# Two units of each attention's output projection beside the attention's end

## The reference, cut to what matters

```python
h = attention(x, ...)                     # concatenated heads o @ w_out, 1024 x 1024
x = layer_norm(ALPHA * x + h, g, b)       # ALPHA = 4 ** 0.25, over the 1024 features
f = conv_ffn(x, ...)
x = layer_norm(ALPHA * x + f, g, b)
```

## Time and profile before

| | us |
|---|---|
| median of 3 runs | 2278.91 |
| lowest, highest | 2278.16, 2282.58 |
| the profiled execution's own time | 2278.12 |
| its span in the trace | 2276.3 |
| PE busy | 2162.4 (95%) |
| mean granted clock of PE | 0.975 of full |

### The profile page before, as it was taken

One profiled execution on the slowest core, in us unless ns is written; L12 is line 12 of the kernel. 1 busy time (PEld: TensorE's weight loads), 2 busy tenths in 40 slices (PEclk: granted clock), 3 DMA queues, 4 the chain that ended last, 5 costly groups with the idle time before them and its releaser, 6 DMA issues.

```text
span 2276.3 us, 27949 instructions
## 1 busy us (share of the span) xinstructions
PE 2162.4 (95%) x10712; PEld 1797.8 (79%) x10720; DVE 1166.1 (51%) x1852; ACT 1005.5 (44%) x2029; POOL 945.9 (42%) x714
## 2 busy tenths in 40 slices
PE   7999899999999898899999999989999999999997
PEld 6888778888877787778888878777678887888886
DVE  3545565544335687565554354676854326444322
ACT  6656444444225666244443245656543334332221
POOL 4555564343447673543433443222413343322233
PEclk9999999999999999999999998999999999999998
DMA  4111122322222321222222212111012222222221
GB/s 176 42 56 58 54 93 95 108 95 102 89 88 79 98 84 38 75 74 93 93 101 94 102 58 75 38 38 38 19 65 93 97 97 72 95 98 106 86 102 54
DMA packets 29844, 183.06 MB, mean 80 GB/s; under 512 B 3984, under 2 KB 4112, under 8 KB 11920
## 3 DMA queue, kind: packets, MB, share of 16 engines
q1 hardware_dynamic: 29712, 181.27, 23.0%
HBM read 174.97 MB, written 2.10 MB: 78 GB/s over the span
## 4 chain that ended last, share of the span: by engine, by line
PE 83%; DVE 7%; ACT 4%; issue 3%; POOL 2%; DMA 1%; SPq 0%; POOLq 0%; DVEq 0%; ACTq 0%
PE PS L1492 81%; PE PS L1617 1%; DVE bQS L2232 1%; PE PS L1730 0%; POOL LO L2783 0%; DMA RAW<-wall 0%; ACT HI L1816 0%; DVE aQS L2232 0%; DVE T_f L2304 0%; DVE bP L2536 0%; DVE YH L2334 0%; PE PS L1665 0%; DVE XL L2309 0%; ACT bQS L2010 0%; POOL cROT L2858 0%
## 5 line engine op out<-in xcount | busy, mean ns | idle before, releaser
L2783 POOL TENSOR_TENSOR LO<-RAW,HI 128x512 fp32r<-128x512 f32 (+2 forms) x382 | 542.4, 1436 | 605.7 <-ACT HI L1816 605.7
L1492 PE MATMUL PS<-XH,HI 128*128 128x512 f32 (+1 forms) x1584 | 637.9, 403 | 23.4 <-DVE XL L2232 7.1
L1492 PE MATMUL PS<-XH,LO 128*128 128x512 f32 (+1 forms) x1584 | 626.0, 395 | 0.0
L1492 PE MATMUL PS<-XL,HI 128*128 128x512 f32 (+1 forms) x1584 | 620.2, 396 | 2.2 <-DVE XL L2309 2.1
L1816 ACT ACTIVATE HI<-RAW 128x512 fp32r<-128x512 f32 (+3 forms) x668 | 366.0, 607 | 171.2 <-PE PS L1492 168.0
L2232 DVE TENSOR_TENSOR LO<-RAW,HI 128x512 fp32r<-128x512 f32 (+2 forms) x286 | 302.5, 1062 | 246.3 <-ACT HI L1816 245.9
L1492 PEld LDWEIGHTS PS<-XH,HI 128*128 128x128 f32 (+1 forms) x1584 | 302.5, 191 | 86.5 <-issue 20.7
L1492 PEld LDWEIGHTS PS<-XH,LO 128*128 128x128 f32 (+1 forms) x1584 | 301.7, 190 | 65.7 <-issue 0.8
L1492 PEld LDWEIGHTS PS<-XL,HI 128*128 128x128 f32 (+1 forms) x1584 | 301.8, 191 | 63.9 <-DVE XL L2309 3.7
L1492 PE MATMUL PS<-HL,HI 128*128 128x512 f32 x528 | 205.6, 389 | 0.0
L1492 PE MATMUL PS<-HH,LO 128*128 128x512 f32 x528 | 205.6, 389 | 0.0
(11 more groups left out here) (404 smaller groups left out, 3307.8 us busy)
## 6 DMA issues: line engine op xcount, KB each, us to landing
RAW<-wall SPq DMA_DIRECT2D x138, 1024.0 KB, 4.8
RAW<-wall SPq DMA_DIRECT2D x24, 896.0 KB, 4.5
bROT<-bTQ SPq DMA_DIRECT2D x64, 64.0 KB, 2.0
RAW<-wall SPq DMA_DIRECT2D x5, 512.0 KB, 3.3
XF<-xT SPq DMA_DIRECT2D x4, 512.0 KB, 5.7
outT<-XR SPq DMA_DIRECT2D x8, 256.0 KB, 2.0
FP<-cfp SPq DMA_DIRECT2D x1, 1024.0 KB, 7.0
MKF<-cmask SPq DMA_DIRECT2D x1, 704.0 KB, 11.2
```

Source lines behind the costliest of these rows:

```text
L1492: return e.matmul(out, a, b, start=start, stop=stop)
L2783: return e.tensor_tensor(out, x, h.bitcast(F32), ALU.subtract)
```

## The change

`lin_begun` now takes two units, `ao 0` and `ao 1` (`bo 0` and `bo 1`). The first unit's chunks go on as before. The second unit's tiles get banks 2 and 3, and its chunks are `m2` steps as well. They are put down at chosen places: by `fill` inside the attention's generators (before `va` (15, 0), and before the first `dno` of a pair of heads), and before the first unit's chunk kk as `spots` says (one before chunk 6 and two before chunk 7 for the first attention, one before 4 and two before 6 for the second). `spare` lets one through only after the last scores of the attention are in the list, and only if the first unit is further along. The chunks that are left follow the first unit. `attn_out` now puts the residuals of all four tiles after both units. The later units' banks rotate from another place.

```diff
+    def fill(n=1):
+        for _ in range(n):
+            if filler[0] is not None:
+                filler[0]()
+
+    def lin_begun(keys, src, last, spots):
+
+        begun, kept, at = [], [None], [0, 0]
+
+        def opened(key, banks):
+            i = take(key)
+            begun.extend((len(tiles), len(tiles) + 1))
+            for j in range(2):
+                tiles.append(Tile([(i, k) for k in range(8)], 128 * j, 128, banks[j], src))
+
+        def second_chunk():
+            if len(begun) < 4:
+                opened(keys[1], (2, 3))
+                kept[0], due[0] = due[0], None
+            step_of_two(begun[2], at[1])
+            at[1] += 1
+
+        def spare():
+            if last in steps and at[1] < at[0]:
+                second_chunk()
+
+        opened(keys[0], [pick(), pick()])
+        filler[0] = spare
+        for kk in range(8):
             if (src, kk) not in ready:
                 until(lambda: (src, kk) in ready)
-        ts = lin_fm(key, src, together=True, before=reached)
+            fill(spots.get(kk, 0))
+            step_of_two(begun[0], kk)
+            at[0] = kk + 1
+            tick()
+            tick()
+        filler[0] = None
         drain()
-        lin["banks"] = [2, 3, 4, 7, 0, 1]
+        if kept[0] is not None:
+            due[0] = kept[0]
+        while at[1] < 8:
+            second_chunk()
+            if kept[0] is not None and due[0] is None:
+                due[0] = kept[0]
+            tick()
+            tick()
+        lin["banks"] = [4, 7, 0, 1, 2, 3]
         lin["n"] = 0
-        return ts
+        return begun
...
+            if h == 15 and kb == 0:
+                fill()
             b, s = 6 + h % 2, ("va", h, kb)
...
-        return lin_begun(("ao", 0), "aO")
+        return lin_begun((("ao", 0), ("ao", 1)), "aO", ("sc", 15, 3), {6: 1, 7: 2})
...
-            for j, t in enumerate(lin_fm((name, i), src) if i else begun):
+            for j, t in enumerate(lin_fm((name, i), src) if i > 1 else begun[2 * i:2 * i + 2]):
                 residual(n, 2 * i + j, t)
...
+                if x == h0:
+                    fill()
                 s, b = put("dno", x, h0, h + 1), flip_bank()
...
-        return lin_begun(("bo", 0), "bO")
+        return lin_begun((("bo", 0), ("bo", 1)), "bO", ("dsc", 7, 3), {4: 1, 6: 2})
```

More of the change, by code:

```diff
@@ L377, in agenda @@
     due = [None, 0.0]
+    filler = [None]
     beside = [None, 0.0, 0.0]
@@ L526, in lin_fm @@
         return list(range(t0, t0 + len(widths)))
-    def lin_begun(key, src):
-        def reached(kk):
+    def fill(n=1):
[21 more added lines that the diff above has]
+        for kk in range(8):
             if (src, kk) not in ready:
                 until(lambda: (src, kk) in ready)
-        ts = lin_fm(key, src, together=True, before=reached)
-        drain()
-        lin["banks"] = [2, 3, 4, 7, 0, 1]
+            fill(spots.get(kk, 0))
[4 more added lines that the diff above has]
+        filler[0] = None
+        drain()
+        if kept[0] is not None:
[7 more added lines that the diff above has]
+        lin["banks"] = [4, 7, 0, 1, 2, 3]
         lin["n"] = 0
-        return ts
+        return begun
     def lin_long(keys, src, evac, last):
```

## The result

| us | before | changed |
|---|---|---|
| median of the runs compared (8 each) | 2279.34 | 2288.53 |
| lowest, highest | 2275.6, 2285.5 | 2282.41, 2294.75 |
| ratio, with its 95% interval | | 1.0037 (1.0021 to 1.0053) |
| the profiled execution's own time | 2278.12 | 2285.02 |
| its span | 2276.3 | 2283.1 |

The change makes the kernel slower by 0.37%, 8.4 us (4.8 to 12.1). The forecast was +10 us.

What follows compares the result with a forecast made beforehand. PE, busy 95% of the span, was taken as the bound. Gains of 3.5 and 6.7 us against waits of 7.4 and 8.2 and 5.0 for the clock gave +10.4, 2289 us against the median of 2278.91; range 2284 to 2293.

Steps and rivals of the forecast that it cites:

- Gain of the filled waits: Attention ends: chunks of the second unit fill PE's waits for DVE, gaining 3.5 us in the first, 6.7 in the second.
- Waits in its place: Unit 2 of the projections: PE waits for late LO pieces, 7.4 us in the first attention, 8.2 in the second.
- Clock: Behind the new waits PE's clock falls to half, costing 2.5 us in each attention, 5.0 together.
- The sign given for it: In the changed profile, a granted clock of 0.50 for some us behind each new wait.
- Rival A: POOL and DVE bring pieces 2 and 3 in time, only the gain of 10.2 is left: 2269 us; chance 0.07.
- line for "faster": The kernel is faster once PE's new waits sum to less than 10.2 us, some 5.1 in each attention.
- Nothing gives this back: Behind the new waits PE has matmuls of units 2 and 3 without waits to fill, so none is recovered.
- Rival B: Waits come, but the clock doesn't fall or POOL's sums run at their lone pace: 2282 to 2284; chance 0.20.
- Rival C: DVE and POOL block one another fully, waits of 9.2 and about 9.5 us: 2292; chance 0.15.
- Rival D: The chunks fill nothing at the attention ends, each delays what it should cover, gain 0: 2299; chance 0.03.
- The banks, priced at nothing: Later units' banks rotate from another place, each still freed units ahead: no cost.
- The DMA: The next load into RAW waits for piece 3 of `ao 2`, yet lands before its first read: no cost.

Runs made afterwards that it cites:

- e1: Changed kernel with what is left of unit 2's split put ahead of the four residuals, in both attentions; ratio to before 1.0020 (1.0007 to 1.0033).
- e7: Changed kernel with only the sums XL + XH moved from DVE to POOL at the attention's end; ratio to before 1.0037 (1.0024 to 1.0051).
- e5: Changed kernel with unit 2's split ahead of later residuals, XL + XH sums moved to POOL, residuals of tiles 0 and 1 behind unit 0; 0.9950 to before, median 2269.2.
- e11: e5 without the chunks in the attention's waits, unit 1 following unit 0 whole; ratio to before 1.0014 (1.0003 to 1.0026).
- e12: Kernel before with only the changed kernel's rotation of PSUM banks from the first feed-forward unit on; ratio to before 1.0007 (0.9995 to 1.0020).
- e9: e5 without its early residuals of tiles 0 and 1; ratio to before 0.9972 (0.9960 to 0.9985).
- e6: Kernel before with only the sums XL + XH moved to POOL at the attention's end; ratio to before 1.0007 (0.9994 to 1.0019).
- e3: The change in the second attention alone, the first as before; ratio to before 1.0049 (1.0034 to 1.0064).
- e4: Changed kernel with piece 3 of unit 2 subtracted by DVE instead of POOL in both attentions; ratio to before 1.0010 (0.9998 to 1.0022).

## Why the prediction was right, and where it was not

- **Gain of the filled waits** (3.5 + 6.7): the waits are gone. Comparing the nth matmul of PE in both profiles, the changed kernel was ahead by 4.0 us more at the end of the first attention than at its last scores, and by 7.0 in the second. Right.
- **Waits in its place** (7.4 + 8.2): 7.83, 2.80 and 5.74, together 16.4. The mechanism, the engines and the place are the forecast ones. DVE's piece came 0.7 sooner than worked out. The near hit for POOL's owes something to luck: in the first attention the six sums took 9.4 us from the first start to the piece's (1.56 each, where 1.32 was put in, so 1.5 more), but they began 0.3 sooner than worked out, and the piece itself took 1.2 and not the 2.0 put in for it beside DVE. The errors cancel to 0.4.
- **Clock** (5.0): 4.0, one fall in each attention, as priced. The sign given for it, a granted clock of 0.50 behind each wait, held for two of the three: behind the wait of 2.80 us the clock stayed at 1.00.
- **The sum**: +10.4 forecast, +8.3 in the stretches, +8.4 in the runs. The four terms as measured make 4.0 + 7.0 = 11.0 gained and 16.4 + 4.0 lost, +9.4, and at the projections' ends the changed kernel is 10.0 us behind. What the stretches show less was given back behind the projections, where the prediction had no term. The upper bound of 2293 takes the gain at 10.2; with the text's own lower gain of 8.7 it is 2295.
- **Rival A, priced wrongly.** The text has it that with pieces 2 and 3 in time "only the gain is left", 2269. e1 made just that true, and it measured 2283.6 where before had 2276.9. The text's own line for "faster", new waits of under 10.2 us in sum, was met as well (7.1), and still the runs show no gain and the stretches only 0.7 us. The text also said that the residuals "can't be earlier"; with the sums XL + XH taken out ahead of them they could (e7: the wait fell from 7.83 to 5.54). The forecast was right for the changed kernel, but its cause was put too narrowly: the order on POOL sets where the wait falls, and the lack of room sets that there is one. The view that would have shown it is POOL's busy time in the windows of this stretch, 28.1 of 32.6 us (86%), not the 42% of the page that the text cites in favour of rival A.
- **"Nothing gives this back"** held up to the layer norms: no wait ahead of them was shortened. Behind them 1.7 us came back in one profile, with the clock.
- **Rival B** (no fall of the clock, or sums at their lone pace): fell, the clock was at 0.50 behind both long waits, and the sums took 1.56 us each and not 1.29. **Rival C** (the engines block one another fully, 9.2 us in the first attention): 7.83 is nearer to the forecast, though POOL's sums did take longer than I had put in. **Rival D** (the chunks fill nothing): refuted by the gone waits, and by e5 against e11.
- **The banks, priced at nothing**: e12 does not contradict it, and can't confirm it to better than some 4 us. The DMA, priced at nothing too: no wait of PE for a load stands in either stretch.

## What to carry to other kernels

Before work is moved into the waits of the engine that bounds the kernel, take the stretch that gets shorter by it and add up the busy time of the other engines in just that stretch: an engine at 42% of the whole was at 86% there, and the saving came back as waits, more than whole in the changed kernel (16.4 us for 11.0) and in large part with the better order of e1 (7.1). Where a list of steps sets the order of all engines, ask for each step that is put down later what then stands in front of it in every queue; here the same chunks gave +8 us with the next weights' split behind the residuals, and -6 (e9) or -11 (e5) with it ahead and eight additions taken out of the stretch. Work whose inputs are known early belongs in the idle time of the attention's end, but moving it pays only together with what needs the room (e6: nothing alone).

## What the runs showed of the hardware that was not expected

- The granted clock in unchanged code differs from one execution to the next by enough to hide a change of this size: 0.99 and 0.96 over the first 240 us, 237.3 and 243.1 us long.
- After a wait of 7.8 us PE came back at half its clock for 2.8 us, less than the 6.5 that the layer norm's gap cost in the earlier trace rows; the length of the wait alone does not give the cost. What else does was not tested.
- Nor does it tell whether the clock falls. The wait of 2.80 us for DVE's piece in the second attention is the same in the changed kernel, e3 and e4, and PE's next 1.5 us ran at 1.00, 0.50 and 0.50. The window of the changed kernel is above; this is e4's:

```profile
947.00:948.50 1.50, 1.46 (x4) 0.50 0.00 0
```

- With DVE's additions of XL and XH gone from the stretch, POOL's copy of a tile took 0.61 us in e5 instead of 1.01. What slowed it before was not tested.
